# Second tile of rows transposed between the two parts of the last tile, its low parts made ahead of the last tile's LayerNorm

## The chip, the cores and the metric

The kernel runs on one core of one Trainium2 chip. Its time is device microseconds (us) of one execution. The kernel before takes 3609.99 us, the median of 3 runs that lie between 3608.74 and 3615.9 us.

## The reference, cut to what matters

Two transformer blocks over 512 rows of 1024 numbers. The first block has two layers, and each layer has three sublayers that end in the same way:

```
x = layer_norm(ALPHA * x + y, ln1_g, ln1_b)      # y: mixer (latent attention and convolution) @ w_o
x = layer_norm(ALPHA * x + y, ln2_g, ln2_b)      # y: attention over 256 rows of memory @ w_o
x = layer_norm(ALPHA * x + y, ln3_g, ln3_b)      # y: (silu(x @ w_g) * (x @ w_up)) @ w_down
```

`layer_norm` takes mean and variance over the 1024 columns of a row. What follows each of them multiplies the new `x` by weights again, so `x` is wanted with its columns on the partitions, that is transposed. After layer 2 the second block begins with an RMS norm of `x` and a wide projection, then window attention, retention, a merge of two branches, a router and 64 experts.

## The kernel before, in words

The 512 rows are four tiles of 128 (i = 0 to 3). `x_tok` holds them with rows on the partitions; `xT` and `xT_low` hold the transposed `x` as a high part, rounded to the format that TensorE multiplies fast, and a low part, the rounding's rest. A product of two such pairs is three matmuls for every 128 of depth (`product`, L617): high by high, high by low, low by high. Weights come in pieces of at most 1 MB through a ring of three slots, and are cut into high (ScalarE) and low (VectorE) in the same way, one piece ahead of TensorE.

Each engine has its own list of instructions, written out by hand in the order of the Python code, and waits on semaphores for named marks of other engines. Nothing is reordered, so a wait holds up everything behind it on that engine.

The end of a sublayer is `project_out_pe` (L725) on TensorE and `project_out_dve` (L759) on VectorE. The output has two halves of 512 columns. Of the second half the last two weight pieces are held together, and their products are issued by tiles of rows: tiles 0 and 1 with both pieces, tile 2 with both, then the callback `turned(0)`, which transposes tile 0, then tile 3 with both pieces. Here the product of tile 3 with the first of the two pieces is called 3a, and with the second 3b. 3a is 12 matmuls; 3b is 12 after the mixer and the cross attention, and 9 after the FFN.

VectorE does for each tile, when its sum is there: the residual add, `bn_stats`, then `norm_dve` (L776): aggregate, argument of the root (the root itself is on GpSimd), and two passes over 128x1024. The second pass gives the mark `normed`. Then comes the callback `after(i)`, which makes the low parts of tile i - 2 (`rows_to_T_dve`, L682, two instructions of 128x512): those of tile 0 behind tile 2's norm, those of tile 1 behind tile 3's norm. Tiles 2 and 3 follow.

A transposed tile is made in three steps: TensorE transposes it into two PSUM banks (`rows_to_T_pe`, L667, eight transposes of 128x128, waits for `normed` of this tile), ScalarE writes the high parts (`rows_to_T_act`, L675), VectorE the low parts. Below, T0 to T3 are TensorE's transposes of tiles 0 to 3.

After the mixer and after the cross attention, T1 and T2 stand behind 3b. Then comes the first piece of the next projection, in two halves of the rows (`two_by_halves_pe`, L644). Each half has two groups of 24 matmuls of 256 columns, one for each 128 output columns: c0 and c1 of the first half of the rows wait for tiles 0 and 1, and T3 stands between them; then come the 48 matmuls of the second half of the rows, which wait for tiles 2 and 3.

After the FFN of layer 1 T1, T2 and T3 stand behind 3b, and then comes the first product of the next mixer, tile after tile. After the FFN of layer 2 there is an RMS norm more for each tile (`square_act` on ScalarE, the root on GpSimd, one pass on VectorE, L1629 and L1636), and it is its result `xn_tok` that is transposed (`xn_turned_pe`, L1529); the projection that follows waits for all four tiles. At the end of the merge in the second block `turned` (L2164) transposes tiles 0 and 1 in one go, and VectorE's callback there is another.

PSUM banks are handed out in the order in which they were given back (`Banks`), and a bank that is taken waits for the mark with which it was given.

Of the kernel before, what the change touches and what calls it, by code (L numbers as in the profile page):

```python
# [18 lines left out]
NT = S // P  # L19
# [171 lines left out]
class Net:  # L191
# [533 lines left out]
    def project_out_pe(self, e, key, label, kt, lhs, lhs_ready, turned=None, behind_first=None):  # L725

        starts = list(range(0, kt, SLOT // BANK))
        for half in range(2):
            for k0 in starts:
                if turned and half and k0 == starts[-2]:  # L730
                    break
                n = self.pe_piece(e, label)
                for i in range(NT):
                    self.out_tile_pe(e, key, kt, lhs, lhs_ready, half, k0, n, i)
                self.release(e, n)
                if behind_first and not half and not k0:
                    behind_first()
        if turned:
            n0, n1 = self.pe_piece(e, label), self.pe_piece(e, label)
            for tiles in ((0, 1), (2,), (3,)):  # L740
                for k0, n in ((starts[-2], n0), (starts[-1], n1)):
                    for i in tiles:
                        self.out_tile_pe(e, key, kt, lhs, lhs_ready, 1, k0, n, i)
                    if tiles[-1] == NT - 1:
                        self.release(e, n)
                if tiles == (2,):
                    turned(0)

# [524 lines left out]
    def cross_pe(self, e, layer):  # L1273
        e.begin(f"cross{layer}")
        l, banks, at = layer, self.banks, self.at
# [7 lines left out]
        def z_back():  # L1283
            for c4 in range(CT):
                bank = banks.take(e, "zb", l, c4)
                for i in range(NT):
# [6 lines left out]
                            lambda k, i: (self.yT[k][:, i * P:(i + 1) * P], self.yT_low[k][:, i * P:(i + 1) * P]),  # L1293
                            lambda k0: [("z_split" if k0 else "y_split", l, k) for k in range(CT)],
                            lambda i: self.rows_to_T_pe(e, f"xT_mix{l}", i, self.x_tok, f"mix{l}", "normed", i), z_back)
        for i in (1, 2):
            self.rows_to_T_pe(e, f"xT_mix{l}", i, self.x_tok, f"mix{l}", "normed", i)

        for j in range(KD // 2):
            n = self.pe_piece(e, "cross query")  # L1300
# [19 lines left out]
        for n in range(len(steps) + 2):  # L1320
            if n < len(steps):
                h, i = steps[n]
# [10 lines left out]
            if 2 <= n:  # L1333
                h, i = steps[n - 2]
# [6 lines left out]
                if i == NT - 1:  # L1341
                    for v in range(2):
# [3 lines left out]
                        for m in range(MT):  # L1346
# [5 lines left out]
                            lambda k, i: (self.oT[:, k, i * P:(i + 1) * P], self.oT_low[:, k, i * P:(i + 1) * P]),  # L1352
                            [("xo_split", l, h, v) for h in range(XH) for v in range(2)],
                            lambda i: self.rows_to_T_pe(e, f"xT_cross{l}", i, self.x_tok, f"cross{l}", "normed", i))
        for i in (1, 2):
            self.rows_to_T_pe(e, f"xT_cross{l}", i, self.x_tok, f"cross{l}", "normed", i)

    def project_out_act(self, e, label, kt, begun=0):
        for _ in range(begun, 2 * len(range(0, kt, SLOT // BANK))):
# [53 lines left out]
    def cross_dve(self, e, layer):  # L1413
        e.begin(f"cross{layer}")
        l, at = layer, self.at
        self.convolve(e, l, self.taps, CT * TAPS)
        for i in range(NT):
            bank = self.bank("zT", l, i)
            e.wait_ge(*at("pe", "zT", l, i))
            e.bn_stats(self.stat[:, i, 0, :], bank[:, :]).then_inc(*e.tick())  # L1420
            e.wait_ge(*e.own())
            e.bn_aggr(self.mean_var[:, i, :], self.stat[:, i, 0, :]).then_inc(*e.tick())
            e.wait_ge(*e.own())
            self.root_dve(e, i, 1, self.mean_var[:, i, 1:2], 1.0, LN_EPS, "z", l, i)
            e.wait_ge(*at("root", "z", l, i))
            e.tensor_scalar(self.v_tok[:, i, :], bank[:, :], self.mean_var[:, i, 0:1], self.root[:, i, 0:1],
                            ALU.subtract, ALU.mult).then_inc(*e.tick("z", l, i))
        self.dve_piece(e, "mix out")
        for c4 in range(CT):
            low = self.yT_low[CT + c4]  # L1430
            e.wait_ge(*at("z_high", l, c4))
            self.low_of(e, low, low, self.yT[CT + c4]).then_inc(*e.tick("z_split", l, c4))
        x_from = (lambda i: ("x_landed",)) if l == 0 else (lambda i: (f"ffn{l - 1}b", "normed", i))
        def turned(i):
            if i >= 2:
                self.rows_to_T_dve(e, f"xT_mix{l}", i - 2, self.xT, self.xT_low)

        self.project_out_dve(e, f"mix{l}", "mix out", KD, ALPHA, True, x_from, turned, begun=1)
        for i in range(2, NT):
            self.rows_to_T_dve(e, f"xT_mix{l}", i, self.xT, self.xT_low)  # L1440
        for j in range(KD // 2):
            self.dve_piece(e, "cross query")
            e.wait_ge(*at("pe", "xq", l, 2 * j))
            e.tensor_copy(self.qT[:, 2 * j, :], self.bank("xq", l, 2 * j)[:, :]).then_inc(*e.tick("xq", l, 2 * j))
        steps = [(h, i) for h in range(XH) for i in range(NT)]
        for n in range(len(steps) + 2):
            if n < len(steps):
                st = self.small[:, 24 + 4 * (n % 4):28 + 4 * (n % 4)]
                e.wait_ge(*at("pe", "xs", l, n))
                e.tensor_reduce(st[:, 0:1], self.bank("xs", l, n)[:, 0:MEM], AX.X, ALU.max).then_inc(*e.tick())  # L1450
                e.wait_ge(*e.own())
                e.tensor_scalar(st[:, 1:2], st[:, 0:1], -(XHD ** -0.5), None, ALU.mult).then_inc(
                    *e.tick("xmax_scaled", l, n))
            if 1 <= n <= len(steps):
                pr, st = self.xprobs[(n - 1) % 4], self.small[:, 24 + 4 * ((n - 1) % 4):28 + 4 * ((n - 1) % 4)]
                e.wait_ge(*at("xp_exp", l, n - 1))
                e.reciprocal(st[:, 3:4], st[:, 2:3]).then_inc(*e.tick())
                e.wait_ge(*e.own())
                e.tensor_scalar(pr, pr, st[:, 3:4], None, ALU.mult).then_inc(*e.tick("xp_scaled", l, n - 1))
            if 2 <= n:  # L1460
                h, i = steps[n - 2]
                if n % 2 == 0:
                    e.wait_ge(*at("pe", "xpT", l, n - 2))
                    e.tensor_copy(self.xprobsT[h % 2][:, :, i * P:(i + 1) * P],
                                  self.bank("xpT", l, n - 2)[:, 0:MEM].rearrange("p (m c) -> p m c", m=MT)).then_inc(
                        *e.tick("xpT", l, n - 2))
                if i == NT - 1:
                    for v in range(2):
                        e.wait_ge(*at("xo_high", l, h, v))
                        self.low_of(e, self.oT_low[:, 2 * h + v, :], self.bank("xo", l, h, v)[:, :],  # L1470
                                    self.oT[:, 2 * h + v, :]).then_inc(*e.tick("xo_split", l, h, v))

        def turned(i):
            if i >= 2:
                self.rows_to_T_dve(e, f"xT_cross{l}", i - 2, self.xT, self.xT_low)

        self.project_out_dve(e, f"cross{l}", "cross out", KD, ALPHA, True, lambda i: (f"mix{l}", "normed", i), turned)
        for i in range(2, NT):
            self.rows_to_T_dve(e, f"xT_cross{l}", i, self.xT, self.xT_low)
# [11 lines left out]
    def ffn_pe(self, e, layer):  # L1491
        e.begin(f"ffn{layer}")
        l, banks = layer, self.banks
        for part, f0, f1 in (("a", 0, FH), ("b", FH, FT)):
            for f in range(f0, f1, 2):
                both = range(f, min(f + 2, f1))
                for label, done in (("ffn gate", "gated"), ("ffn up", "hid")):
# [9 lines left out]
                    for c in both:  # L1507
                        bank = banks.take(e, label, l, c)
                        e.wait_ge(*self.piece_ready(n))
                        for mark in self.x_marks(f"xT_cross{l}"):  # L1510
# [6 lines left out]
                                lambda k, i: (self.hidT[:, k, i * P:(i + 1) * P], self.hidT_low[:, k, i * P:(i + 1) * P]),  # L1517
                                [("hid_split", l, c) for c in range(f0, f1)],
                                (lambda i: self.ffn_turned_pe(e, l, i)) if part == "b" else None)
        for i in range(1, NT):  # L1520
            self.ffn_turned_pe(e, l, i)

    def ffn_turned_pe(self, e, l, i):
# [56 lines left out]
    def ffn_dve(self, e, layer):  # L1580
        e.begin(f"ffn{layer}")
        l, at = layer, self.at
        for part, f0, f1 in (("a", 0, FH), ("b", FH, FT)):
# [12 lines left out]
            if part == "a":  # L1596
                self.project_out_dve(e, f"ffn{l}a", "ffn down", f1 - f0, ALPHA, False,
                                     lambda i: (f"cross{l}", "normed", i))
            else:
                def turned(i):  # L1600
                    if l + 1 == DEPTH and i:
                        self.rms_dve(e, i - 1, self.xn_tok[:, i - 1, :], self.mix_gain, "mix_norm", ("mix_gain_landed",))
                    if i >= 2:
                        split(i - 2)

                def split(i):
                    if l + 1 < DEPTH:
                        self.rows_to_T_dve(e, f"xT_ffn{l}", i, self.xT, self.xT_low)
                    else:
                        self.xn_turned_dve(e, i)  # L1610

                self.project_out_dve(e, f"ffn{l}b", "ffn down", f1 - f0, 1.0, True,
                                     lambda i: (f"ffn{l}a", "added", 1, i), turned)
                if l + 1 == DEPTH:
                    self.rms_dve(e, NT - 1, self.xn_tok[:, NT - 1, :], self.mix_gain, "mix_norm", ("mix_gain_landed",))
                for i in range(2, NT):
                    split(i)
# [521 lines left out]
    def merge_pe(self, e):  # L2139
# [4 lines left out]
        for c0, branch in self.merge_groups():  # L2144
# [17 lines left out]
                banks.give(("m_branch", branch, c), "m_half", branch, c)  # L2162
            self.release(e, n)
        def turned(i):  # L2164
            for n, slot in enumerate(self.early_slots):
                self.add_slot(f"early{n}", slot, "pe", "m_branch", "retention", KD - 1)
            for j in (0, 1):
                self.rows_to_T_pe_f32(e, j)
# [739 lines left out]
```

## Time and profile before

| | |
|---|---|
| median of 3 runs | 3609.99 us |
| the profiled execution | 3611.64 us |
| its span, first to last instruction | 3609.8 us |
| TensorE busy | 3285.5 us, 91% of the span |
| VectorE busy | 1323.4 us, 37% |
| ScalarE busy | 871.3 us, 24% |
| GpSimd busy | 161.7 us, 4% |
| TensorE's mean granted clock | 0.953 |
| share of TensorE in the chain that ended last | 68% |
| share of DMA and of VectorE in that chain | 16% and 9% |

Times in the rows are us from the span's start. Engines are PE (TensorE matmul), PEld (its weight load), DVE (VectorE), ACT (ScalarE), POOL (GpSimd). A number in square brackets at a row's end is the time for which the engine stood idle before the row, and what ended it. Matmuls overlap: their pace is the distance of their starts, not their duration.

### The profile page before, as it was taken

What the parts mean: (1) busy time and instruction counts of PE and PEld (TensorE: products, weight loads), DVE (VectorE), ACT (ScalarE), POOL (GpSimd) and SP (SyncE); (2) the same over time, 40 slices, a digit from 0 to 9 for tenths busy, and PEclk for the clock granted to TensorE, in tenths of its full rate; (3) what the DMA queues carried; (4) which work ended last, traced back from release to release, by engine and by line L of the source; (5) the groups of instructions that cost most, each with busy time, mean ns of one, the idle gap of its engine ahead of it and who ended that gap; (6) DMA issues with size and microseconds to landing.
All of it is one profiled execution on the core that took longest, in us unless ns stands there. A gap on an engine that the chain in (4) does not pass through costs nothing.

```text
span 3609.8 us, 36003 instructions
## 1 busy us (share of the span) xinstructions
PE 3285.5 (91%) x15200; PEld 2252.0 (62%) x15200; DVE 1323.4 (37%) x2235; ACT 871.3 (24%) x1383; POOL 161.7 (4%) x146
## 2 busy tenths in 40 slices
PE   6998899999998899998999989899699999999994
PEld 5667688887667678886888866677433333333331
DVE  3575353335576443235344344533311111111112
ACT  2342322222243322122233331122111111111111
POOL 0110000001010000000100000000100000000001
PEclk9999999999999999998999999999799999999997
DMA  4112122333112123232211321023499999999996
GB/s 150 47 59 94 59 82 91 102 102 104 59 59 94 56 74 102 91 105 95 70 53 53 90 76 65 30 94 134 198 423 423 422 423 422 423 423 422 423 421 245
DMA packets 229400, 627.55 MB, mean 174 GB/s; under 512 B 14801, under 2 KB 136401, under 8 KB 179825
## 3 DMA queue, kind: packets, MB, share of 16 engines
q1 hardware_dynamic: 207312, 579.37, 41.9%
q10 hardware_dynamic: 19728, 37.68, 2.9%
q0 software_dynamic: 2192, 8.13, 0.8%
q8 instruction: 122, 2.00, 0.2%
q14 instruction: 46, 0.37, 0.0%
HBM read 600.23 MB, written 22.81 MB: 173 GB/s over the span
## 4 chain that ended last, share of the span: by engine, by line
PE 68%; DMA 16%; DVE 9%; ACT 3%; POOL 2%; issue 2%; ACTq 0%; DVEq 0%; POOLq 0%
PE bank L120 66%; DMA piece<-in_moe_w 4%; DMA mT_slot<-in_moe_w 3%; DMA piece_high<-in_moe_w 3%; PE bank L123 2%; DMA xT<-in_moe_w 2%; DVE x_tok L138 1%; POOL root L135 1%; DVE gate_acc L138 1%; DMA norm_room<-in_moe_w 1%; DMA memT<-in_moe_w 1%; DMA y_att_slot<-in_moe_w 1%; DVE stat L153 1%; DVE piece_rounded L135 1%; ACT piece_high_rounded L126 1%
## 5 line engine op out<-in xcount | busy, mean ns | idle before, releaser
L120 PE MATMUL bank<-xT_rounded,piece_high_rounded 128*128 128x512 f32 (+1 forms) x1408 | 549.2, 390 | 25.7 <-DVE xT_low_rounded L135 25.7
L135 DVE TENSOR_TENSOR piece_rounded<-piece,piece_high_rounded 128x2048 fp32r<-128x2048 f32 (+1 forms) x156 | 342.1, 2198 | 573.4 <-ACT piece_high_rounded L126 573.2
L120 PE MATMUL bank<-xT_low_rounded,piece_high_rounded 128*128 128x512 f32 (+1 forms) x1408 | 539.6, 383 | 0.0
L120 PE MATMUL bank<-xT_rounded,piece_rounded 128*128 128x512 f32 (+1 forms) x1408 | 539.5, 383 | 0.0
L135 DVE TENSOR_TENSOR gate_and_hidden<-gate_and_hidden,bank 64x512 f32<-64x512 f32 x64 | 69.2, 1081 | 844.5 <-ACT gate_and_hidden L126 844.5
L126 ACT ACTIVATE piece_high_rounded<-piece 128x2048 fp32r<-128x2048 f32 (+1 forms) x156 | 282.9, 1820 | 291.3 <-DMA piece<-in_ffn_w_down 116.2
L120 PEld LDWEIGHTS bank<-xT_rounded,piece_high_rounded 128*128 128x128 f32 x1408 | 270.0, 192 | 81.7 <-DVE xT_low_rounded L135 27.0
L120 PEld LDWEIGHTS bank<-xT_low_rounded,piece_high_rounded 128*128 128x128 f32 x1408 | 269.7, 192 | 53.2 <-issue 4.1
L120 PEld LDWEIGHTS bank<-xT_rounded,piece_rounded 128*128 128x128 f32 x1408 | 269.5, 191 | 50.5
L120 PE MATMUL bank<-piece,xeT 128*64 128x512 f32 x488 | 237.7, 641 | 20.5 <-DMA piece<-in_moe_w 9.2
L120 PE MATMUL bank<-piece_high,xeT 128*64 128x512 f32 x464 | 184.5, 631 | 16.6 <-DMA piece<-in_moe_w 12.8
L120 PE MATMUL bank<-xT,xeT 128*64 128x512 f32 x312 | 158.7, 657 | 13.2 <-DMA piece_high<-in_moe_w 7.1
L120 PE MATMUL bank<-piece_high_rounded,xT_rounded 128*128 128x192 f32 (+1 forms) x448 | 150.2, 335 | 18.3 <-issue 16.5
L138 DVE SCALAR_TENSOR_TENSOR gate_acc<-hT,cols,gate_acc 128x512 f32<-128x512 f32 x240 | 163.2, 743 | 0.0
L120 PE MATMUL bank<-mT_slot,xeT 128*64 128x512 f32 x304 | 151.6, 654 | 9.7 <-DMA piece_high<-in_moe_w 9.7
L126 ACT ACTIVATE gate_and_hidden<-bank 64x512 f32<-64x512 f32 x64 | 37.8, 590 | 507.5 <-PE bank L120 507.5
L120 PE MATMUL bank<-piece_high_rounded,hidT_rounded 128*128 128x512 f32 x352 | 139.7, 397 | 9.0 <-DVE hidT_low_rounded L135 9.0
L120 PE MATMUL bank<-piece_rounded,xT_rounded 128*128 128x192 f32 (+1 forms) x448 | 146.4, 327 | 0.0
L120 PE MATMUL bank<-piece_high_rounded,xT_low_rounded 128*128 128x192 f32 (+1 forms) x448 | 146.4, 327 | 0.0
L120 PE MATMUL bank<-piece_high_rounded,hidT_low_rounded 128*128 128x512 f32 x352 | 139.0, 395 | 0.0
L120 PE MATMUL bank<-piece_rounded,hidT_rounded 128*128 128x512 f32 x352 | 138.8, 394 | 0.0
L135 POOL TENSOR_TENSOR root<-root,power 128x1 f32<-128x1 f32 (+2 forms) x60 | 60.9, 1016 | 1460.1 <-DVE root L132 1460.1
(337 smaller groups left out, 5142.7 us busy)
## 6 DMA issues: line engine op xcount, KB each, us to landing
piece<-in_moe_w SPq DMA_DIRECT2D x90, 1024.0 KB, 16.7
piece_high<-in_moe_w SPq DMA_DIRECT2D x88, 1024.0 KB, 16.9
xT<-in_moe_w SPq DMA_DIRECT2D x59, 1024.0 KB, 16.9
mT_slot<-in_moe_w SPq DMA_DIRECT2D x58, 1024.0 KB, 17.0
piece<-in_ffn_w_in SPq DMA_DIRECT2D x40, 1024.0 KB, 5.2
memT<-in_moe_w SPq DMA_DIRECT2D x30, 1024.0 KB, 16.4
y_att_slot<-in_moe_w SPq DMA_DIRECT2D x30, 1024.0 KB, 16.9
norm_room<-in_moe_w SPq DMA_DIRECT2D x29, 1024.0 KB, 17.0
```

What stands on the lines that cost most here:

```text
L120: return self.engine.matmul(*a, **k) if self.engine is not None else Nothing()
L123: return self.engine.transpose(*a, **k) if self.engine is not None else Nothing()
L126: return self.engine.activation(*a, **k) if self.engine is not None else Nothing()
L135: return self.engine.tensor_tensor(*a, **k) if self.engine is not None else Nothing()
L138: return self.engine.scalar_tensor_tensor(*a, **k) if self.engine is not None else Nothing()
L153: return self.engine.bn_stats(*a, **k) if self.engine is not None else Nothing()
```

## The change

`project_out_pe` calls its callback a second time, as `turned(1)`, after 3a and the release of its weight piece, ahead of 3b. The loops behind the projections then start with tile 2. On VectorE the callbacks make the low parts of tiles 0 and 1 both behind tile 2's norm, and nothing behind tile 3's. The merge's callback returns at once when it is called with 1. The number of instructions of each kind is the same.

```diff
@@ project_out_pe
                     if tiles[-1] == NT - 1:
                         self.release(e, n)
+                        if k0 == starts[-2]:
+                            turned(1)
                 if tiles == (2,):
                     turned(0)
@@ cross_pe, behind the mixer's projection (and the same behind the cross attention's)
-        for i in (1, 2):
-            self.rows_to_T_pe(e, f"xT_mix{l}", i, self.x_tok, f"mix{l}", "normed", i)
+        self.rows_to_T_pe(e, f"xT_mix{l}", 2, self.x_tok, f"mix{l}", "normed", 2)
@@ cross_dve, mixer (and the same for cross)
         def turned(i):
-            if i >= 2:
-                self.rows_to_T_dve(e, f"xT_mix{l}", i - 2, self.xT, self.xT_low)
+            if i == 2:
+                for j in (0, 1):
+                    self.rows_to_T_dve(e, f"xT_mix{l}", j, self.xT, self.xT_low)
@@ ffn_pe
-        for i in range(1, NT):
+        for i in (2, 3):
             self.ffn_turned_pe(e, l, i)
@@ ffn_dve
                 def turned(i):
                     if l + 1 == DEPTH and i:
                         self.rms_dve(e, i - 1, self.xn_tok[:, i - 1, :], self.mix_gain, "mix_norm", ("mix_gain_landed",))
-                    if i >= 2:
-                        split(i - 2)
+                    if i == 2:
+                        for j in (0, 1):
+                            split(j)
@@ merge_pe
         def turned(i):
+            if i:
+                return
             for n, slot in enumerate(self.early_slots):
```

## Rows read from the trace of the kernel before

**Rows 1.** Waits of TensorE: total us, times, longest us.
```profile
PE bank L120 <- DVE xT_low_rounded L135: 25.7, 5, 6.1
```
**Rows 2.** Timeline, TensorE, cross attention of layer 1 into its FFN: start, us.
```profile
470.55 1.04 PE L123 MATMUL bank<-ident,x_tok 128*128 128x128 f32 x8
...
476.91 1.98 PE L123 MATMUL bank<-ident,x_tok 128*128 128x128 f32 x16
484.95 0.55 PE L120 MATMUL bank<-xT_rounded,piece_high_rounded 128*128 128x256 f32 x1 [6.06 <-DVE xT_low_rounded L135]
...
490.21 1.37 PE L123 MATMUL bank<-ident,x_tok 128*128 128x128 f32 x8
491.33 0.36 PE L120 MATMUL bank<-xT_rounded,piece_high_rounded 128*128 128x256 f32 x1
...
494.29 0.28 PE L120 MATMUL bank<-xT_rounded,piece_high_rounded 128*128 128x256 f32 x1
```
**Rows 3.** Timeline, VectorE, the same stretch.
```profile
471.78 1.28 DVE L138 SCALAR_TENSOR_TENSOR x_tok<-x_tok,root,norm_room 128x1024 f32<-128x1024 f32 x1 [0.44 <-POOL root L135]
...
477.66 1.28 DVE L135 TENSOR_TENSOR xT_low_rounded<-bank,xT_rounded 128x512 fp32r<-128x512 f32 x2
478.86 0.68 DVE L138 SCALAR_TENSOR_TENSOR x_tok<-x_tok,bank 128x512 f32<-128x512 f32 x1
...
483.52 2.48 DVE L135 TENSOR_TENSOR xT_low_rounded<-bank,xT_rounded 128x512 fp32r<-128x512 f32 x4
491.81 1.29 DVE L135 TENSOR_TENSOR xT_low_rounded<-bank,xT_rounded 128x512 fp32r<-128x512 f32 x2 [5.81 <-ACT xT_rounded L126]
```
**Rows 4.** Timeline, ScalarE, the same stretch: the high parts of tile 0.
```profile
471.19 1.09 ACT L126 ACTIVATE xT_rounded<-bank 128x512 fp32r<-128x512 f32 x2 [9.79 <-PE bank L123]
```
**Rows 5.** Timeline, TensorE, the three like places: c0's start and T3.
```profile
340.09 0.55 PE L120 MATMUL bank<-xT_rounded,piece_high_rounded 128*128 128x256 f32 x1 [6.06 <-DVE xT_low_rounded L135]
...
344.81 1.03 PE L123 MATMUL bank<-ident,x_tok 128*128 128x128 f32 x8
...
1168.90 0.55 PE L120 MATMUL bank<-xT_rounded,piece_high_rounded 128*128 128x256 f32 x1 [6.06 <-DVE xT_low_rounded L135]
...
1173.90 1.04 PE L123 MATMUL bank<-ident,x_tok 128*128 128x128 f32 x8
...
1315.74 0.55 PE L120 MATMUL bank<-xT_rounded,piece_high_rounded 128*128 128x256 f32 x1 [6.06 <-DVE xT_low_rounded L135]
...
1320.70 1.04 PE L123 MATMUL bank<-ident,x_tok 128*128 128x128 f32 x8
```
**Rows 6.** Timeline, FFN of layer 1 into the mixer: T2, T3; VectorE's low parts.
```profile
859.50 1.97 PE L123 MATMUL bank<-ident,x_tok 128*128 128x128 f32 x8 [2.56 <-DVE x_tok L138]
865.36 1.97 PE L123 MATMUL bank<-ident,x_tok 128*128 128x128 f32 x8 [3.89 <-DVE x_tok L138]
...
865.22 3.67 DVE L135 TENSOR_TENSOR xT_low_rounded<-bank,xT_rounded 128x512 fp32r<-128x512 f32 x6
```
**Rows 7.** Timeline, FFN of layer 2 into attention: T1; VectorE's steps.
```profile
1695.18 1.03 PE L123 MATMUL bank<-ident,xn_tok 128*128 128x128 f32 x8
...
1692.15 1.29 DVE L138 SCALAR_TENSOR_TENSOR xn_tok<-x_tok,root,mix_gain 128x1024 f32<-128x1024 f32 x1 [0.65 <-POOL root L135]
...
1695.38 0.69 DVE L138 SCALAR_TENSOR_TENSOR x_tok<-x_tok,bank 128x512 f32<-128x512 f32 x1 [0.74 <-PE bank L120]
...
1702.05 1.28 DVE L135 TENSOR_TENSOR xT_low_rounded<-bank,xT_rounded 128x512 fp32r<-128x512 f32 x2
...
1704.05 1.28 DVE L138 SCALAR_TENSOR_TENSOR xn_tok<-x_tok,root,mix_gain 128x1024 f32<-128x1024 f32 x1 [0.66 <-POOL root L135]
```
**Rows 8.** Stretches: us, then busy us (count) of PE, PEld, DVE, ACT, POOL; PEclk; DMA share; GB/s.
```profile
485.00:490.20 5.20, 5.20 (x24) 5.20 (x25) 1.00 (x2) 0.00 (x0) 0.00 (x0) 0.50 0.00 0
...
1306.00:1308.50 2.50, 1.02 (x9) 0.78 (x7) 2.06 (x3) 1.09 (x2) 1.22 (x1) 1.00 1.08 369
...
1309.70:1315.70 6.00, 0.00 (x0) 0.00 (x0) 5.46 (x10) 0.67 (x2) 1.51 (x1) 0.53 0.22 68
```

More of the change, by code:

```diff
@@ L1354, in cross_pe @@
                             lambda i: self.rows_to_T_pe(e, f"xT_cross{l}", i, self.x_tok, f"cross{l}", "normed", i))
-        for i in (1, 2):
-            self.rows_to_T_pe(e, f"xT_cross{l}", i, self.x_tok, f"cross{l}", "normed", i)
+        self.rows_to_T_pe(e, f"xT_cross{l}", 2, self.x_tok, f"cross{l}", "normed", 2)
     def project_out_act(self, e, label, kt, begun=0):
@@ L1473, in turned @@
         def turned(i):
-            if i >= 2:
-                self.rows_to_T_dve(e, f"xT_cross{l}", i - 2, self.xT, self.xT_low)
+            if i == 2:
+                for j in (0, 1):
+                    self.rows_to_T_dve(e, f"xT_cross{l}", j, self.xT, self.xT_low)
         self.project_out_dve(e, f"cross{l}", "cross out", KD, ALPHA, True, lambda i: (f"mix{l}", "normed", i), turned)
@@ L1602, in turned @@
                         self.rms_dve(e, i - 1, self.xn_tok[:, i - 1, :], self.mix_gain, "mix_norm", ("mix_gain_landed",))
-                    if i >= 2:
-                        split(i - 2)
+                    if i == 2:
+                        for j in (0, 1):
+                            split(j)
                 def split(i):
```

## The prediction

> **What bounds the kernel now.** I read the page's busy shares first: TensorE is busy for 91% of the span and carries 68% of the chain that ended last, so a microsecond in which it stands idle or runs slowly in the first half of the program is a microsecond of the result, unless something later waits for a fixed supply. Then the waits of TensorE. One line is about the data that the change touches: it waits for low parts of `xT` 5 times, 25.7 us in total [rows 1]. Four of these five are 6.06 us each, at the same point of the mixer's and the cross attention's ends in both layers [rows 2, 5], and 25.7 - 24.2 = 1.5 us are left for the fifth, where attention begins. So I read one of the four places on all engines.
>
> In [rows 2] TensorE issues T0 at 470.55, then 3a and 3b, then T1 and T2 together from 476.91, and is done with them at 484.95 - 6.06 = 478.89. c0 starts only at 484.95. In [rows 3] VectorE is busy without a gap over that time: it starts the low parts of tile 0 at 477.66 and tile 3's residual add at 478.86; tile 3's norm fills the time up to 483.52; then come the low parts of tiles 1 and 2 (four instructions, 2.48 us). c0 wants those of tile 1. They are the first two of the four, 1.20 us, so they end at 484.72, and c0 starts 0.23 us later. The wait is VectorE's order: tile 1's low parts stand behind a whole LayerNorm of 483.52 - 478.86 = 4.66 us, which they don't need. TensorE's T1, just behind 3b, isn't late for that order, only for the new one.
>
> **The four places behind mixer and cross attention.** Let L be the start of tile 0's low parts (477.66 here). The new order on VectorE is low 0 (L to L + 1.20), low 1 (to L + 2.40), tile 3's add and norm (to L + 7.06), low 2, low 3. Can low 1 run at L + 1.20? T1 is issued behind 3a. From T0 (470.55) to T1 (476.91) are T0's own 0.8 us and 24 matmuls, 5.56 us together, so 3a ends about 474.1; tile 1's `normed` is there at 471.78 + 1.28 = 473.06 [rows 2, 3]. High parts begin 0.64 us behind the transposes' start and take 1.09 us (T0: 470.55 to 471.19) [rows 2, 4], so for tile 1 they end at 475.9, 3.0 us ahead of 478.86. VectorE doesn't wait. T1 pushes 3b back by 0.8 us, to an end of about 477.7; its sum is wanted at L + 2.40 = 480.06, so this costs nothing: VectorE is the one that is behind.
>
> c0 then starts 0.23 us behind low 1, at L + 2.63 against L + 7.29 now: 4.66 us earlier, and the idle time ahead of it falls from 6.06 to 1.40 us. That is not yet the gain, for T3 is next and waits for tile 3's norm, which now ends 1.20 us later. From [rows 6]: T3 starts 0.14 us behind the VectorE instruction that follows the norm (865.36 against 865.22), so here at L + 7.06 + 0.14 = L + 7.20.
>
> What does c0 take? Now it runs slowly: (490.21 - 484.95) / 24 = 0.219 us for each matmul in [rows 2], at a granted clock of 0.50, which is the lower of the two levels, 1.2 GHz [rows 8]; c1, 24 matmuls with T3's tail gone, takes 494.29 - 491.33 = 2.96 us, 0.123 each. With c0 at the upper level it ends at L + 5.6, and TensorE waits 1.6 us for T3. With c0 at the lower it would end at L + 7.9. So T3's start is set by VectorE, at L + 7.20. Taking L = c0's start now less 7.29, T3 moves as follows [rows 2, 5]: 344.81 to 340.00 (4.81 us), 490.21 to 484.86 (5.35), 1173.90 to 1168.81 (5.09), 1320.70 to 1315.65 (5.05): 20.3 us. At the second place T3 itself still ran partly at the lower level, 1.12 us to the next start against about 0.8, so 0.3 us more: 20.6 us.
>
> Is the rest in time? The second half of the rows needs low 3. It starts 491.81 - 490.21 = 1.60 us behind T3 and takes 1.29, so T3 + 2.9; T3 with c1 takes 0.8 + 2.96 = 3.8 us. Nothing waits, with 0.9 us to spare. Low 2 runs at L + 7.06 to L + 8.26, ahead of low 3. The first piece of the weight ring that is freed (behind 3a) is freed as now; the second is freed 0.8 us later, and its reader comes two pieces on, over 9 us of matmuls at these rates. No DMA is added. Banks: T1 takes two whose owners, half 0 of tiles 2 and 3, were added long before; only T1's and tile 3's change places in the list. Bound of both edits: 0 to 0.8 us a place; I take 0.
>
> **The FFN of layer 1.** No product of half rows stands here that could use tile 1 early. VectorE again has no gap, and low 1 moves ahead of tile 3's norm, so `normed` of tile 3 and T3 come 1.20 us later, 866.56 instead of 865.36 [rows 6]. T3 is in TensorE's list ahead of the mixer's first product, so this is a loss: 1.2 us, or 0.6 if the matmuls behind it, now at the lower level, reach the upper one at the same moment as before. I take 1.2.
>
> **The FFN of layer 2.** 3b is 9 matmuls at 0.227, so 3a ends at 1695.18 - 2.05 = 1693.13. T1 wants tile 1's RMS pass, done at 1692.15 + 1.28 = 1693.43 [rows 7]: it waits 0.3 us, and with its 0.8 us 3b ends near 1696.5, and tile 3's add starts 1.3 us later than 1695.38. The high parts of tile 1 end 0.64 + 1.09 us behind T1's start, at 1695.2, so low 1 is done near 1696.1, inside this time. Behind tile 3's norm low 1 is gone from 1702.05, which gives 1.20 us back ahead of tile 3's RMS pass (1704.05). Loss 0.1 us; bounds 0 to 0.6. The merge does the same work as before.
>
> **Sum.** 20.6 - 1.2 - 0.1 = 19.3 us. The profiled execution is 3611.64 us, its span 3609.8 us; the difference stays. That gives 3592.3 us against this execution, which is 1.65 us above the median, and 3590.7 against the median. I say 3591.5 us.
>
> **What the clock may do.** In the new order TensorE has two short idles close together, 1.40 us ahead of c0 and 1.6 us ahead of T3. In [rows 8] the clock was still at its upper level through 1306.00 to 1308.50, where TensorE was busy for 1.02 of 2.50 us; but then, with T2 of 1.1 us behind that, it fell almost at once in the idle stretch from 1309.70 (mean 0.53 over 6 us). In [rows 6] T2, behind an idle of 2.56 us that followed only T1's transposes, ran 1.97 us, the lower level. So an idle of less than 3 us can be enough, when only transposes lie around it. Between the new idles stand 2.9 us of dense matmuls, which is more, so I take the upper level. The Trainium skill, "TensorE: Matmul & The Clock Gate", section "A second HAM failure mode: psum-queue depth-cycling", says that idles too short to look harmful can, when frequent, make the clock swing between its levels. It speaks against this change, and gives the second case below.
>
> **Rivals.**
> (A) As summed: 3591.5 us, own range 3588 to 3595. 65%.
> (B) The lower level catches c0, T3 and c1. c0 ends at L + 7.9, 0.7 us late for T3; T3 takes 0.8 us more and c1 24 x (0.219 - 0.123) = 2.3 us more: 3.8 us of the 5.15 us that a place gives. At all four places: 19.3 - 15.2 = 4.1 us gained, 3606; at half of them 3599. For it: the two idles and [rows 6]. Against: c0's dense matmuls. 22%, most of it near 3599.
> (C) The wait doesn't move: something else releases c0, such as its weight piece, and the four places stay: 1.3 us lost, 3611.5. Against: the 0.23 us between low 1 and c0 at the place read, and four waits equal to 0.01 us. 8%.
> (D) Slower: the lower level doesn't end with c1 but lasts on through the second half of the rows. These are 48 matmuls, 48 x 0.096 = 4.6 us more a place. It decides from the 14th of them, where the rest of 1.35 us is used up; at full length it is 4 x (3.8 + 4.6 - 5.15) + 1.3 = 14 us lost, 3624. Against: now, after 6 us of idle, c0 takes 4.72, 5.00 and 4.96 us at three places against 5.26 at the fourth [rows 2, 5], so the upper level is back before c0 ends. 5%.
>
> **How the numbers follow.** A measurement of this kernel can tell about 0.2%, 7 us, from no change. A and nearly all of B lie beyond it: faster 87%. C and the far end of B: same 9%. D: slower 4%. The range reaches from a clock that is also kept up at the FFN, 3587, to B at three places, 3603.
>
> **What would show it.** The waits of TensorE for `xT` low parts should fall from 25.7 to about 7 us, four of 1.4 us; new waits of about 1.6 us ahead of T3 in the mixer's and cross attention's ends; c0 of 2.9 us instead of 5.3, at a granted clock near 1; tile 1's two low parts right behind tile 0's. T3 behind the first FFN should come 1.2 us later relative to T2. I am wrong if c0 or T3 is released by ScalarE's high parts of tile 1, or if c1 takes over 4 us.

## The result, and the profile after

The changed kernel takes 3588.26 us, the median of 6 runs (3583.56 to 3593.51); the kernel before, with three runs more beside them, takes 3609.31 (3608.14 to 3615.9). That is 21.1 us less, a ratio of 0.9941 with a 95% interval of 0.9930 to 0.9951. Forecast were 3591.5 us and a range of 3587 to 3603.

The profiled execution of the changed kernel is its fastest, 3583.56 us with a span of 3581.8, so the two profiles lie 28.0 us apart in their spans and not 21. Where the difference arises can be read at one place, the start of the attention projection, where the first block ends. TensorE's first instruction and this start (1708.86 before) are 14.43 and 1708.86 us before, and 14.63 and 1687.69 after: 1694.43 us against 1673.06, 21.4 us less. The rest, up to the end of the span, is 1900.9 us before and 1894.1 after. Both kernels do the same work there, and the 6.8 us aren't the change's: the executions profiled below took 1893.6 to 1900.7 us for it. Over this stretch TensorE was busy for 1708 us in the two executions that took 1900.7 us and more, and for 1690 to 1698 us in the other eight, with the same 8156 matmuls.

The waits of TensorE for low parts of `xT` (us in total, times, longest), which stood at 25.7 us [rows 1], in the changed kernel:

```profile
PE bank L120 <- DVE xT_low_rounded L135: 7.2, 5, 1.6
```

The end of the cross attention of layer 1, on TensorE (start, us; the answer to [rows 2]): T0, T1 ahead of 3b, T2, c0, T3, c1.

```profile
463.82 1.03 PE L123 MATMUL bank<-ident,x_tok 128*128 128x128 f32 x8
...
467.45 1.03 PE L123 MATMUL bank<-ident,x_tok 128*128 128x128 f32 x8
...
471.06 1.03 PE L123 MATMUL bank<-ident,x_tok 128*128 128x128 f32 x8
473.45 0.36 PE L120 MATMUL bank<-xT_rounded,piece_high_rounded 128*128 128x256 f32 x1 [1.36 <-DVE xT_low_rounded L135]
...
478.03 1.09 PE L123 MATMUL bank<-ident,x_tok 128*128 128x128 f32 x8 [1.47 <-DVE x_tok L138]
478.88 0.36 PE L120 MATMUL bank<-xT_rounded,piece_high_rounded 128*128 128x256 f32 x1
```

VectorE over the same stretch (the answer to [rows 3]): the second pass of tile 2's norm, the four low parts of tiles 0 and 1 in one row, tile 3's add, the second pass of its norm, the low parts of tile 2 and of tile 3.

```profile
469.63 1.29 DVE L138 SCALAR_TENSOR_TENSOR x_tok<-x_tok,root,norm_room 128x1024 f32<-128x1024 f32 x1 [0.44 <-POOL root L135]
470.83 2.48 DVE L135 TENSOR_TENSOR xT_low_rounded<-bank,xT_rounded 128x512 fp32r<-128x512 f32 x4
473.22 0.68 DVE L138 SCALAR_TENSOR_TENSOR x_tok<-x_tok,bank 128x512 f32<-128x512 f32 x1
...
476.69 1.28 DVE L138 SCALAR_TENSOR_TENSOR x_tok<-x_tok,root,norm_room 128x1024 f32<-128x1024 f32 x1 [0.44 <-POOL root L135]
477.89 1.28 DVE L135 TENSOR_TENSOR xT_low_rounded<-bank,xT_rounded 128x512 fp32r<-128x512 f32 x2
479.35 1.29 DVE L135 TENSOR_TENSOR xT_low_rounded<-bank,xT_rounded 128x512 fp32r<-128x512 f32 x2 [0.18 <-ACT xT_rounded L126]
```

L is 470.83 here. c0 starts at L + 2.62, forecast L + 2.63; T3 at L + 7.20, forecast L + 7.20. c0 and the wait behind it take 478.03 - 473.45 = 4.58 us, and it is the same at the three like places (c0's start and T3, the answer to [rows 5]):

```profile
335.14 0.36 PE L120 MATMUL bank<-xT_rounded,piece_high_rounded 128*128 128x256 f32 x1 [1.39 <-DVE xT_low_rounded L135]
339.72 1.09 PE L123 MATMUL bank<-ident,x_tok 128*128 128x128 f32 x8 [1.47 <-DVE x_tok L138]
...
1153.81 0.36 PE L120 MATMUL bank<-xT_rounded,piece_high_rounded 128*128 128x256 f32 x1 [1.39 <-DVE xT_low_rounded L135]
1158.39 1.09 PE L123 MATMUL bank<-ident,x_tok 128*128 128x128 f32 x8 [1.47 <-DVE x_tok L138]
...
1294.97 0.36 PE L120 MATMUL bank<-xT_rounded,piece_high_rounded 128*128 128x256 f32 x1 [1.40 <-DVE xT_low_rounded L135]
1299.55 1.09 PE L123 MATMUL bank<-ident,x_tok 128*128 128x128 f32 x8 [1.47 <-DVE x_tok L138]
```

From T2's end to T3's start was 6.06 us of wait and 4.72, 5.26, 5.00 and 4.96 us of c0 [rows 2, 5]; it is now 1.39, 1.36, 1.39 and 1.40 us of wait and 4.58 us. The differences are 4.81, 5.38, 5.09 and 5.04 us, 20.3 in all. From T0's start to T3's the four places became 21.0 us shorter (19.64, 19.66, 19.42 and 21.05 before; 14.50, 14.21, 14.39 and 15.68 after); where the other 0.7 us come from is told under "The sum". The clock stays up in c0 (stretches with busy us and count of PE, PEld, DVE, ACT and POOL, then PEclk; the answer to [rows 8]):

```profile
335.00:338.20 3.20, 3.06 (x24) 2.93 (x24) 2.84 (x5) 0.00 (x0) 1.37 (x1) 1.00 0.65 229
...
473.40:476.50 3.10, 3.05 (x24) 2.93 (x24) 2.75 (x5) 0.00 (x0) 1.36 (x1) 1.00 0.76 265
```

Behind the FFN of layer 1, T2 and T3 (the answer to [rows 6]):

```profile
846.89 1.09 PE L123 MATMUL bank<-ident,x_tok 128*128 128x128 f32 x8 [1.50 <-DVE x_tok L138]
853.96 1.97 PE L123 MATMUL bank<-ident,x_tok 128*128 128x128 f32 x8 [5.97 <-DVE x_tok L138]
```

From T2 to T3 it takes 7.07 us, where it took 5.86: the 1.2 us that were forecast as a loss.

### The profile page after: what moved, and what is told of

It is laid out like the page before. It is cut to its first block, busy times and chain, and to the rows that moved or that the text cites. A ratio compares the mean times of both kernels' runs of the same rounds, so it can differ in the third digit from the quotient of the medians.

```text
span 3581.8 us, 36003 instructions
## 1 busy us (share of the span) xinstructions
PE 3261.2 (91%) x15200; PEld 2236.9 (62%) x15200; DVE 1327.6 (37%) x2235; ACT 872.3 (24%) x1383; POOL 163.0 (5%) x146
## 4 chain that ended last, share of the span: by engine, by line
PE 67%; DMA 17%; DVE 9%; ACT 3%; POOL 2%; issue 2%; ACTq 0%; DVEq 0%; POOLq 0%
PE bank L120 65%; DMA piece<-in_moe_w 4%; DMA piece_high<-in_moe_w 3%; DMA mT_slot<-in_moe_w 3%; DMA xT<-in_moe_w 3%; PE bank L123 2%; DVE x_tok L138 1%; POOL root L135 1%; DVE gate_acc L138 1%; DMA y_att_slot<-in_moe_w 1%; DMA memT<-in_moe_w 1%; DMA norm_room<-in_moe_w 1%; DVE stat L153 1%; DVE piece_rounded L135 1%; ACT piece_high_rounded L126 1%
## 5 line engine op out<-in xcount | busy, mean ns | idle before, releaser
L120 PE MATMUL bank<-mT_slot,xeT 128*64 128x512 f32 x304 | 149.7, 648 | 10.6 <-DMA piece_high<-in_moe_w 10.6
L120 PEld LDWEIGHTS bank<-piece,xeT 128*64 128x64 f32 x488 | 69.6, 148 | 93.6 <-issue 93.6
```

The source lines that it names most:

```text
L120: return self.engine.matmul(*a, **k) if self.engine is not None else Nothing()
```

## The experiments

Beside each time stands what the trace says up to the start of attention, from TensorE's first instruction; one execution each, but without the second block's scatter. The kernel before took 3610.76 us beside e1 to e4 and 3610.23 beside a1 and e5 to e7.

| kernel | median us | ratio to before, 95% | to the start of attention, us |
|---|---|---|---|
| before | 3609.31 | | 1694.4 |
| changed | 3588.26 | 0.9941 (0.9930 to 0.9951) | 1673.1 |
| changed, again (a1) | 3585.29 | 0.9936 (0.9919 to 0.9952) | 1674.1 |
| e1, VectorE's half | 3588.41 | 0.9940 (0.9923 to 0.9957) | 1677.7 |
| e2, TensorE's half | 3608.75 | 0.9998 (0.9989 to 1.0008) | 1696.9 |
| e3, four places only | 3586.90 | 0.9938 (0.9921 to 0.9955) | 1671.4 |
| e4, stall filled | 3600.11 | 0.9974 (0.9961 to 0.9986) | 1684.7 |
| e5, add in the gap | 3582.73 | 0.9921 (0.9904 to 0.9937) | 1668.1 |
| e6, T3 inside | 3582.75 | 0.9930 (0.9913 to 0.9946) | 1665.1 |
| e7, e5 and e6 | 3573.23 | 0.9904 (0.9887 to 0.9921) | 1659.0 |

**e1: only VectorE's half.** Edit against before: the callbacks of `cross_dve` and `ffn_dve`, nothing on TensorE.

```diff
-            if i >= 2:
-                self.rows_to_T_dve(e, f"xT_mix{l}", i - 2, self.xT, self.xT_low)
+            if i == 2:
+                for j in (0, 1):
+                    self.rows_to_T_dve(e, f"xT_mix{l}", j, self.xT, self.xT_low)
@@ cut: the same for xT_cross, and with split(j) in ffn_dve
```

> Only VectorE's half of the change: the low parts of tiles 0 and 1 stand behind tile 2's norm, TensorE's order is that of before (T1 behind 3b). Theory V (the order on VectorE alone is the cause): the high parts of tile 1 end 1.7 us behind T1's start, at 333.3, 478.6, 1162.6 and 1307.7 us of the trace of before, and low 1 would start at 334.0, 478.9, 1162.8 and 1309.7, so VectorE doesn't wait for them; c0 starts 4.7 us earlier as in the changed kernel, waits of TensorE for xT low parts about 7 us in total, time 3587 to 3592, within noise of the changed kernel's 3588.3. At the end of the second FFN VectorE waits for tile 1's high parts, 0.4 us more than in the changed kernel. Theory P (T1 must come early): low 1 waits, the norm of tile 3 slips with it, 3600 to 3609 us.

It measured 3588.41 us. TensorE's rows at the cross attention's end: T0, T1 and T2 in one row behind 3b, c0, T3.

```profile
466.64 1.03 PE L123 MATMUL bank<-ident,x_tok 128*128 128x128 f32 x8
...
472.98 2.17 PE L123 MATMUL bank<-ident,x_tok 128*128 128x128 f32 x16
476.54 0.36 PE L120 MATMUL bank<-xT_rounded,piece_high_rounded 128*128 128x256 f32 x1 [1.39 <-DVE xT_low_rounded L135]
481.12 1.09 PE L123 MATMUL bank<-ident,x_tok 128*128 128x128 f32 x8 [1.48 <-DVE x_tok L138]
```

c0's wait and the 4.58 us to T3 are those of the changed kernel, with T1 where it was before. Theory V holds at the four places, and P falls. At the end of the second FFN the wait was forecast too small. VectorE's low parts of tile 0, of tile 1, and tile 3's add there:

```profile
1675.54 1.28 DVE L135 TENSOR_TENSOR xT_low_rounded<-bank,xT_rounded 128x512 fp32r<-128x512 f32 x2
1678.75 1.29 DVE L135 TENSOR_TENSOR xT_low_rounded<-bank,xT_rounded 128x512 fp32r<-128x512 f32 x2 [1.92 <-ACT xT_rounded L126]
1679.95 0.68 DVE L138 SCALAR_TENSOR_TENSOR x_tok<-x_tok,bank 128x512 f32<-128x512 f32 x1
```

VectorE waits 1.92 us for tile 1's high parts, against 0.18 us for them and 0.59 for the sum in the changed kernel: 1.15 us more, where 0.4 was expected. This place alone has something of T1's early turn. From T0 to the start of attention it takes 23.2 us in e1, and 21.9 and 22.2 in the changed kernel's two profiles, about 1 us more. That is a part only of the 4.6 us by which e1's profile stands behind in the table: 3.0 of them lie ahead of the first place, where the two kernels do the same.

**e2: only TensorE's half.** T1 ahead of 3b (`project_out_pe` and the loops behind it, and the merge's early return); VectorE as before.

> Only TensorE's half of the change: T1 ahead of 3b, VectorE's order that of before. Theory V: four waits of 6.06 us for xT low parts stay, nothing is gained, and at the end of the second FFN 3b ends 1.1 us later: 3609 to 3611 us. Theory P: most of the 21 us, 3588 to 3595.

It measured 3608.75 us, a ratio of 0.9998. The same place: T1, T2, c0, T3.

```profile
475.73 1.04 PE L123 MATMUL bank<-ident,x_tok 128*128 128x128 f32 x8
...
479.37 1.04 PE L123 MATMUL bank<-ident,x_tok 128*128 128x128 f32 x8
486.42 0.55 PE L120 MATMUL bank<-xT_rounded,piece_high_rounded 128*128 128x256 f32 x1 [6.01 <-DVE xT_low_rounded L135]
...
491.68 1.41 PE L123 MATMUL bank<-ident,x_tok 128*128 128x128 f32 x8
```

The wait is whole. With e1, this settles that the gain at the four places is the order on VectorE. At the end of the second FFN e2 loses: from T0 to the start of attention it takes 23.4 us, where three profiles with the order of before (before, e3, e4) take 22.0, 22.1 and 21.2. T1 makes tile 3's add later there, and tile 1's low parts still stand ahead of tile 3's RMS pass.

**e3: the four places only.** The changed kernel with both FFN ends as before.

```diff
-                                (lambda i: self.ffn_turned_pe(e, l, i)) if part == "b" else None)
-        for i in (2, 3):
+                                (lambda i: self.ffn_turned_pe(e, l, i) if i == 0 else None) if part == "b" else None)
+        for i in range(1, NT):
@@ cut: in ffn_dve, split(i - 2) behind the norms of tiles 2 and 3 as before
```

> The change at the four places behind mixer and cross attention, both FFN ends as before. Theory V with my working: the wait ahead of T3 at the end of the first FFN is 3.9 us again instead of 6.0 with T2's wait apart, T3 comes 1.2 us sooner behind T2, and 1.3 us are gained over the changed kernel: 3587, inside the noise of its runs (3583.6 to 3593.5), so it is read from the trace. A rival (the FFN ends gain as well, since 21.0 us were measured and 19.3 forecast): T3 there comes no sooner, 3589 to 3592.

It measured 3586.90 us, which is no different from the changed kernel by time. T2 and T3 behind the first FFN:

```profile
848.13 1.09 PE L123 MATMUL bank<-ident,x_tok 128*128 128x128 f32 x8 [2.58 <-DVE x_tok L138]
854.00 1.97 PE L123 MATMUL bank<-ident,x_tok 128*128 128x128 f32 x8 [4.77 <-DVE x_tok L138]
```

5.87 us from T2 to T3, against 7.07: the loss of 1.2 us at this place is the change's, as worked out. The waits were stated wrongly in the expectation (3.9 us "again"): it is 4.77 here, since T2, at the upper level this time, is over sooner. To the start of attention e3 is 1.6 us ahead of the changed kernel's one profile and 2.6 ahead of its other.

**e4: the stall filled.** The kernel before, with 48 matmuls of 256 columns ahead of c0's wait, into c1's bank, which c1 then starts afresh.

```diff
+                        if half == 0 and c == 0 and (i, b) == (0, 0):
+                            w_ = self.piece_cols(n, 0, 2 * P)
+                            for m in range(48):
+                                x_ = self.rounded(w_(m % KD)[0])
+                                e.matmul(banks[1][:, 0:2 * P], x_[:, 0:P], x_, start=True, stop=True)
                         e.wait_ge(*self.at(key, i, b))
```

> The kernel before, with 48 more matmuls of 256 columns ahead of c0 at each of the four places (into the bank that c1 starts afresh), so that TensorE works while it waits for tile 1's low parts: the wait stays, only the clock is kept up. c0's start stays where it is and c0 takes 2.9 us instead of 4.7 to 5.3, 8.1 us over the four places: 3601 us, if the clock is a part of what each stall costs. If the change gains by the idle time alone, c0 takes as long as before: 3609.

It measured 3600.11 us. c0 and T3 at the cross attention's end, and the stretch with the filler in it:

```profile
483.46 0.36 PE L120 MATMUL bank<-xT_rounded,piece_high_rounded 128*128 128x256 f32 x1 [0.31 <-DVE xT_low_rounded L135]
486.41 1.04 PE L123 MATMUL bank<-ident,x_tok 128*128 128x128 f32 x8
```
```profile
477.00:483.00 6.00, 6.00 (x52) 5.94 (x50) 5.46 (x9) 1.18 (x3) 1.52 (x1) 1.00 0.61 196
```

c0 takes 2.95 us at each of the four places, 11.8 us where it was 19.9: 8.1 us less over the four, with nothing but a busy TensorE over the same wait. That is 2.0 us at each place, so a stall costs 6.06 us of idle time and 2.0 us more in the matmuls behind it. The change doesn't get both in full: it takes 4.7 us of idle time and the 2.0 us, and pays 1.5 us in the new wait ahead of T3. By time e4 gained 10.6 us, 2.5 more than c0 explains. 1.7 of them are at the fourth place: there c0 starts 14.35 us behind T0 in e4 and 16.09 before, since low 0 starts sooner (see "The sum"). The rest lies within the scatter.

**a1: the changed kernel again.**

> The changed kernel once more, beside the next three on the same chip. Its runs so far lie between 3583.6 and 3593.5 us, those of before closer together; if the spread comes from where the clock's lower level falls, each profile will show other stretches of it, and the sum of their lengths goes with the time at about half a microsecond for each microsecond. 3588 us.

Its median is 3585.29 us (3584.15 to 3588.72) on another chip than e1 to e4. The rule of a half doesn't fit the times. The mean granted clock of the changed kernel's six first runs is 0.962, 0.962, 0.961, 0.958, 0.958 and 0.955 at 3583.6, 3586.4, 3589.9, 3586.6, 3590.5 and 3593.5 us. A microsecond at the lower level lowers the mean clock as half a microsecond at none would, so by the rule the difference of 0.007, of 3590 us, would be 25 us between the ends, and 10 were measured. Much of the lower level may fall where TensorE waits for something else; that wasn't read from the traces. Two sources of scatter in the first block can be read, and stand under "The sum"; what else makes it stays open.

**e5: the add in the gap.** The changed kernel; the norm of tile i (0 or 1) does the residual add of tile i + 1 between its two passes, while GpSimd takes the root.

```diff
                                op0=ALU.subtract, op1=ALU.mult).then_inc(*e.tick(key, "gained", i))
+        if between:
+            between()
         e.wait_ge(*self.at("root", key, i))
@@ cut: between is add_dve of tile i + 1 without its bn_stats, which follow behind norm i
```

> The changed kernel, and on VectorE the residual add of tiles 1 and 2 in the 0.43 us in which the norm of tiles 0 and 1 waits for GpSimd's root. If VectorE's chain of norms sets T3 (my theory), T3 comes 0.87 us sooner at the four places and at the first FFN's end: 4.3 us in all, 3584 us. If TensorE or ScalarE sets it, nothing comes of it: 3588.

It measured 3582.73 us. T0, T2, c0 and T3 at the cross attention's end, and the start of tile 0's low parts:

```profile
465.74 1.04 PE L123 MATMUL bank<-ident,x_tok 128*128 128x128 f32 x8
...
473.00 1.04 PE L123 MATMUL bank<-ident,x_tok 128*128 128x128 f32 x8
474.31 0.36 PE L120 MATMUL bank<-xT_rounded,piece_high_rounded 128*128 128x256 f32 x1 [0.28 <-DVE xT_low_rounded L135]
478.89 1.09 PE L123 MATMUL bank<-ident,x_tok 128*128 128x128 f32 x8 [1.47 <-DVE x_tok L138]
```
```profile
471.69 2.48 DVE L135 TENSOR_TENSOR xT_low_rounded<-bank,xT_rounded 128x512 fp32r<-128x512 f32 x4
```

L is 5.95 us behind T0, where it was 470.83 - 463.82 = 7.01: 1.06 us sooner. T3 stays at L + 7.20, and c0's wait goes from 1.4 to 0.3 us (0.3 to 1.0 at the four places). VectorE's chain of norms sets T3, as my theory had it. To the start of attention it is 5 to 6 us ahead of the changed kernel, a little more than the 4.3 expected.

**e6: T3 inside the next product.** The changed kernel; behind the first FFN T3 is issued ahead of tile 2 of the mixer's first product.

```diff
         for i in range(NT):
+            if l and i == 2:
+                self.rows_to_T_pe(e, x_key, NT - 1, self.x_tok, f"ffn{l - 1}b", "normed", NT - 1)
             bank = banks.take(e, "c", l, i)
@@ cut: the product waits for both low parts of tile i; behind layer 1's FFN only T2 is left of the loop over (2, 3)
```

> The changed kernel, with T3 behind the first FFN issued inside the mixer's first product, behind its tiles 0 and 1, rather than ahead of it. The FFN's end then uses the early low parts of tile 1: the product starts 2.6 us behind the start of tile 0's low parts instead of 8.8, its first 24 matmuls fill 5.5 us of the wait of 6.0 us, and the clock has no reason to fall: 6 to 7.5 us less, 3581 us. If the loss at that place wasn't the order but something in the mixer behind it (its loads, for which ScalarE waits), T3's new place gives under 2 us.

It measured 3582.75 us (3576.47 to 3587.38). T2, the product's start, T3, and tile 2's product; then the clock over the stretch behind:

```profile
850.27 1.09 PE L123 MATMUL bank<-ident,x_tok 128*128 128x128 f32 x8 [1.50 <-DVE x_tok L138]
851.55 0.47 PE L120 MATMUL bank<-piece_high_rounded,xT_rounded 128*128 128x512 f32 x1 [0.20 <-DVE xT_low_rounded L135]
...
857.33 1.09 PE L123 MATMUL bank<-ident,x_tok 128*128 128x128 f32 x8
858.62 0.47 PE L120 MATMUL bank<-piece_high_rounded,xT_rounded 128*128 128x512 f32 x1 [0.20 <-DVE xT_low_rounded L135]
```
```profile
851.50:862.00 10.50, 10.18 (x47) 8.10 (x48) 7.72 (x12) 3.15 (x5) 1.51 (x1) 1.00 0.32 96
```

The wait of 5.97 us ahead of T3 is gone, the product starts 1.28 us behind T2's start (the changed kernel: T3 at 853.96 is already 7.07 behind it), and the clock stays up. By time the gain over a1 is 2.5 us with runs 11 us apart, less than expected; to the start of attention it is 8.9 us against a1 and 7.9 against the first profile, a little more than expected. Most of it is at this place: from T0 behind the first FFN to T0 behind the next mixer it takes 297.3 us, 306.3 and 306.2 in the two profiles of the changed kernel, and 304.3 before. e7 shows it once more (297.4 us).

**e7: both.**

> Both of these. They act on different waits, but at the first FFN's end the add in the gap is worth little once T3 has work around it: 3.5 + 6.5 us, 3578 us.

It measured 3573.23 us (3568.87 to 3578.67), 12.1 us under a1 on the same chip and 37.0 under the kernel before that was run beside it (3610.23); its interval against before, 0.9887 to 0.9921, just touches that of a1 (0.9919 to 0.9952). To the start of attention it is 1659.0 us, 15.0 under a1, the sum of e5's and e6's 5.9 and 8.9. This is the fastest version found.

## Why the prediction was right

**What bounds.** Right. The one line of the waits that was picked fell from 25.7 to 7.2 us, forecast about 7, and e2 shows that the same wait stays whole when only TensorE's list changes. One reading was not exact: VectorE was not busy "without a gap", for in each norm it waits 0.43 or 0.44 us for the root [rows 3]. It changes nothing in the sum, and e5 is built on it.

**The four places.** Right to 0.1 us, reckoned from L: c0 at L + 2.62 for L + 2.63, T3 at L + 7.20 for L + 7.20, 20.3 us in all for 20.3, and the 0.3 us of T3's slow tail at the second place (0.85 us to the next start, where it was 1.12). That the limit moves from tile 1's low parts to tile 3's norm was the step that mattered: the wait alone would have given 18.7 us over the four places (6.06 to 1.39, 1.36, 1.39 and 1.40), and the wait with the slow c0, as e4 splits them, 18.7 + 8.1 = 26.8. Low 3 came in time: it ends at 479.35 + 1.29 = 480.6, 2.6 us behind T3's start, and T3 with c1 takes about 3.7 us.

**T1's turn ahead of 3b.** Bounded at 0 to 0.8 us a place and taken as 0; e1 shows 0 at the four places from the other side, for without it nothing is lost there.

**The FFN ends.** The first: 1.20 us lost was forecast, 1.21 measured from T2 to T3, and e3 takes it back. The second: 0.1 us was forecast. From T0 to attention's start it is 21.9 us in the changed kernel (1665.76 to 1687.69) and 22.0 before (1686.83 to 1708.86). In the changed kernel's other profile it is 22.2. The later add (9.9 us behind T0 where it was 8.6) and the low parts that no longer stand ahead of tile 3's RMS pass cancel (17.4 us behind T0 where it was 17.2), as they were worked out; e1 and e2, with one half of the change each, take about 1 us more. These are its T0, T1, T2 with T3 and the start of attention:

```profile
1665.76 1.97 PE L123 MATMUL bank<-ident,xn_tok 128*128 128x128 f32 x8 [6.40 <-DVE xn_tok L138]
...
1672.43 1.10 PE L123 MATMUL bank<-ident,xn_tok 128*128 128x128 f32 x8
...
1682.47 3.59 PE L123 MATMUL bank<-ident,xn_tok 128*128 128x128 f32 x16 [6.87 <-DVE root L132]
1687.69 0.47 PE L120 MATMUL bank<-xT_rounded,piece_high_rounded 128*128 128x512 f32 x1 [1.64 <-DVE xT_low_rounded L135]
```

**The clock, rival B.** It didn't come: c0 ran at the upper level at all four places, in every profile that has the new order. What the Trainium skill says of short, frequent idles ("TensorE: Matmul & The Clock Gate", section "A second HAM failure mode: psum-queue depth-cycling") did not show here with two idles at a place, of 1.4 and 1.5 us, around 2.9 us of dense matmuls. The clock did count in the old stalls: e4 shows that it was 2.0 us of each one's price.

**Rivals C and D.** C is excluded by the wait's fall to 1.4 us. D is excluded by the clock: behind the first place's T3, from 339.8 to 463.8 us, it is 1.00 throughout, and where c0, T3 and c1 run at the upper level there is no lower level to last on.

**The sum.** 19.3 us were forecast. 21.4 were seen up to the start of attention and 21.1 by time, with 20.4 in a1's profile. The interval of the ratio is 17.7 to 25.3 us, so the time alone can't tell 19.3 from 21.1. By the rows, the 21.4 us are 21.0 from T0 to T3 at the four places, 1.05 lost from T0 to T3 behind the first FFN (1.2 from T2 to T3), 1.6 gained between the first and the second place, 0.9 lost between the first FFN and the third place, and what is under 0.3 us each. The 1.6, the 0.9 and 0.7 of the 21.0 are not the change's. What is left for it is 20.3 + 0.3 - 1.2 + 0.1 = 19.5 us, and the forecast of 19.3 is right by these terms; what the 21.1 us have beyond it is not the change's, as far as the rows tell. Between the first two places the trace of before has a short stretch at the lower level that the changed kernel's has not; the same work, before and after:

```profile
420.00:436.00 16.00, 12.42 (x41) 7.12 (x40) 7.38 (x17) 7.30 (x11) 0.00 (x0) 0.89 0.21 66
```
```profile
414.00:430.00 16.00, 12.41 (x46) 7.59 (x45) 8.80 (x18) 7.30 (x11) 0.00 (x0) 1.00 0.23 66
```

With the clock at 1.00 all the way from T3 of the first place to T0 of the second (changed, a1, e1, e3, e4) it takes 124.1 us, with such a stretch in it 125.5 to 125.8 (before, e2, e5), and with a longer one 127.2 (e6). Ahead of the third place it is the other way round, 0.91 before (1117 to 1137 us) and 0.83 after (1106 to 1126).

The 0.7 us are L, which comes 0.3 us sooner behind T0 at the first and at the fourth place, and 0.1 at the second. At the fourth place the reason can be read. ScalarE waits there for a weight piece of the FFN from DMA, and VectorE's chain of norms begins behind it; before and after:

```profile
1290.28 1.92 ACT L126 ACTIVATE piece_high_rounded<-piece 128x2048 fp32r<-128x2048 f32 x1 [10.55 <-DMA piece<-in_ffn_w_in]
```
```profile
1274.17 1.92 ACT L126 ACTIVATE piece_high_rounded<-piece 128x2048 fp32r<-128x2048 f32 x1 [10.28 <-DMA piece<-in_ffn_w_in]
```

L is 18.2 us behind this row in both (1308.45 and 1292.35), and also in a1, e1, e3 and e4, while from T0 to L it takes 8.8, 8.5, 8.0, 8.7, 7.8 and 7.1 us. So at this place the landing of a weight piece sets L and, 7.2 us later, T3 of the changed kernel, and it moved by up to 1.7 us between these executions.

## What to carry to other kernels

When a wait goes, look for the chain that the waiting work feeds, not only for the one that it waits on: here 4.7 us of wait and 2.0 us of slow clock gave 5.1 us, because tile 3's norm came next. Before an instruction is moved ahead on one engine, ask which list is the late one. TensorE's half of this change did nothing at the four places; at the end of the second FFN it cost about 1 us by itself, and kept about 1 us from being lost beside the other half. And a step that helps where its result is used early costs where it isn't, until the consumer is rearranged as well: with T3 inside the next product the way from the first FFN's T0 to the next mixer's became 9 us shorter than in the changed kernel, and 7 shorter than before.

## What the runs showed of the hardware that was not expected

- Two idles of nearly the same length ended at different levels of the clock. T2 behind the first FFN, after 2.56 us of idle, ran 1.97 us before [rows 6]; after 2.58 us in e3 (above), e1 and e4 it ran 1.09 us. TensorE's instructions ahead of it were the same. A single such row doesn't tell what an idle of this length costs.
- GpSimd's root over 128x1 takes 1.51 us while VectorE runs the first pass of the LayerNorm over 128x1024, and 0.54 us when VectorE waits for it, in the RMS norm. Two such rows of the kernel before, a LayerNorm's root and an RMS norm's:

```profile
1681.94 1.51 POOL L135 TENSOR_TENSOR root<-root,power 128x1 f32<-128x1 f32 x1 [3.15 <-DVE root L132]
1684.91 0.54 POOL L135 TENSOR_TENSOR root<-root,power 128x1 f32<-128x1 f32 x1 [1.46 <-DVE root L132]
```

The gap of 0.44 us in each LayerNorm may thus be made in part by VectorE's own instruction ahead of it; no run tested that.
